# Key norm of the gated delta rule issued beside the value tiles' projections, value silus behind it

## Reference

```python
def gated_deltanet(q, k, v, z, a, b_logit, conv_w, a_log, dt_bias, norm_w):
    qkv = jax.nn.silu(causal_dwconv(jnp.concatenate([q, k, v], axis=-1), conv_w))
    q, k, v = jnp.split(qkv, 3, axis=-1)
    q = l2norm(to_chunks(q)) * D ** -0.5
    k = l2norm(to_chunks(k))
    v = to_chunks(v)
    ...
    sol = lax.linalg.triangular_solve(lower, rhs, left_side=True, lower=True, unit_diagonal=True)
    ...
    _, o = lax.scan(step, jnp.zeros((bsz, H, D, D), f32), xs)
```

## Time and profile before

| | us |
|---|---|
| timed runs | 3829.78, 3832.85, 3834.25 (median 3832.85) |
| the profiled execution's own time | 3828.58 |
| its span | 3826.8 |
| TensorE busy | 3475.4 (91% of the span) |
| VectorE / ScalarE / GpSimd busy | 47% / 34% / 11% |
| mean granted TensorE clock | 0.949 of full speed |
| mixer of the first layer, key norm's first sum to the last round's end | 1902.4 to 2093.5 |
| mixer of the second layer, the same | 2905.6 to 3093.5 |

### The profile page before, as it was taken

One profiled execution on the slowest core, in us unless ns is written; L12 is line 12 of the kernel. 1 busy time (PEld: TensorE's weight loads), 2 busy tenths in 40 slices (PEclk: granted clock), 3 DMA queues, 4 the chain that ended last, 5 costly groups with the idle time before them and its releaser, 6 DMA issues. The chain is left out here.

```text
span 3826.8 us, 46458 instructions
## 1 busy us (share of the span) xinstructions
PE 3475.4 (91%) x19317; PEld 2705.3 (71%) x19317; DVE 1780.1 (47%) x2762; ACT 1308.2 (34%) x2038; POOL 420.6 (11%) x351
## 2 busy tenths in 40 slices
PE   5989897999999789998897988999989988899998
PEld 4877765788777567886665756788766665577886
DVE  4775465443332534332544454444444444554534
ACT  2332353223232332322422353333333134533333
POOL 0001000120000101100023000221001310013100
PEclk7999998999999899999899999999989989999999
DMA  6651215333221032331301103232122020213231
GB/s 228 199 175 45 78 34 187 118 124 110 90 75 55 1 132 69 105 109 35 99 18 27 37 1 110 87 100 101 66 76 61 2 63 1 88 55 110 77 110 50
DMA packets 230575, 316.69 MB, mean 83 GB/s; under 512 B 13133, under 2 KB 167606, under 8 KB 229086
## 3 DMA queue, kind: packets, MB, share of 16 engines
q1 hardware_dynamic: 230366, 313.72, 24.9%
HBM read 311.04 MB, written 6.85 MB: 83 GB/s over the span
## 5 line engine op out<-in xcount | busy, mean ns | idle before, releaser
L493 PE MATMUL out<-h_lo,w_hi 128*128 128x512 f32 x2608 | 1043.1, 400 | 52.1 <-DVE w_lo L484 47.8
L494 PE MATMUL out<-h_hi,w_hi 128*128 128x512 f32 x2608 | 1022.2, 392 | 0.0
L495 PE MATMUL out<-h_hi,w_lo 128*128 128x512 f32 x2608 | 1021.6, 392 | 0.0
L484 DVE TENSOR_TENSOR w_lo<-ring,w_hi 128x1024 fp32r<-128x1024 f32 (+2 forms) x459 | 560.7, 1227 | 980.0 <-ACT w_hi L479 974.9
L479 ACT ACTIVATE w_hi<-ring 128x1024 fp32r<-128x1024 f32 (+2 forms) x459 | 469.2, 1027 | 1152.9 <-PE out L495 1061.1
L493 PEld LDWEIGHTS out<-h_lo,w_hi 128*128 128x128 f32 x2608 | 494.0, 189 | 178.1 <-issue 60.4
L494 PEld LDWEIGHTS out<-h_hi,w_hi 128*128 128x128 f32 x2608 | 493.8, 189 | 111.9 <-issue 11.0
L495 PEld LDWEIGHTS out<-h_hi,w_lo 128*128 128x128 f32 x2608 | 493.6, 189 | 103.9
L493 PE MATMUL item_banks<-h_lo,w_hi 128*128 128x512 f32 (+1 forms) x632 | 289.4, 458 | 14.3 <-DVE w_lo L484 5.1
L494 PE MATMUL item_banks<-h_hi,w_hi 128*128 128x512 f32 (+1 forms) x632 | 255.1, 404 | 0.0
L495 PE MATMUL item_banks<-h_hi,w_lo 128*128 128x512 f32 (+1 forms) x632 | 254.8, 403 | 0.0
(11 more groups left out here) (499 smaller groups left out, 4635.8 us busy)
## 6 DMA issues: line engine op xcount, KB each, us to landing
ring<-in_mlp_w SPq DMA_DIRECT2D x30, 2048.0 KB, 8.5
ring<-in_w_up SPq DMA_DIRECT2D x44, 1024.0 KB, 7.4
tiles<-in_mod_w SPq DMA_DIRECT2D x80, 512.0 KB, 4.6
ring<-in_e_w_in SPq DMA_DIRECT2D x48, 512.0 KB, 4.1
ring<-in_w_down SPq DMA_DIRECT2D x10, 2048.0 KB, 7.7
ring<-in_w_in SPq DMA_DIRECT2D x16, 1024.0 KB, 5.2
ring<-in_o_w_in SPq DMA_DIRECT2D x7, 2048.0 KB, 7.9
tiles<-in_mod_w SPq DMA_DIRECT2D x8, 1024.0 KB, 8.8
```

Of the source, the lines that this page charges most:

```text
L484: return nc.vector.tensor_tensor(lo.bitcast(F32R), x, hi, ALU.subtract)
L493: nc.tensor.matmul(out, wh, xl, start=start, stop=False, **kw)
L494: nc.tensor.matmul(out, wh, xh, start=False, stop=False, **kw)
L495: return nc.tensor.matmul(out, wl, xh, start=False, stop=stop, **kw)
```

## The change

Four numbers of the plan are changed. `DELTA` is 87.5 and no longer 94. The key norm begins 3.5 behind the last key item (67.9 and no longer 84.7) and is spread over 15.5 and no longer 9.0. The silus of the three value tiles are planned 3.0, 3.7 and 4.4 behind the last conv item, and no longer 3.0 behind each tile's own end. Since the item length changes from 5.6 to 9.4 at `DELTA`, the last item now ends at 167.6, and rotary follows at 168.6 (before 164.8). No arithmetic operation is added or taken away.

```diff
@@ Item.__init__
-        self.begin, self.length = 0.0, 0.0
+        self.begin, self.length, self.silu_at = 0.0, 0.0, None
@@ items_lane, ScalarE
-                steps += [(end, 2, m), (end + 3.0, 3, m)]
+                steps += [(end, 2, m), (end + 3.0 if item.silu_at is None else item.silu_at, 3, m)]
@@ second_mixer
-        BEGIN, DELTA, ROUND = 18.0, 94.0, 28.0
+        BEGIN, DELTA, ROUND = 18.0, 87.5, 28.0
...
+        keys_end, conv_end = (items[TC + n * GDN_T - 1].begin + items[TC + n * GDN_T - 1].length for n in (2, 3))
+        for t in range(GDN_T):
+            items[TC + 2 * GDN_T + t].silu_at = conv_end + 3.0 + 0.7 * t
...
-            conv_end = items[12].begin + items[12].length
-            normed = key_norm_lane(k, r, r.lane(conv_end + 3.5, 9.0),
+            normed = key_norm_lane(k, r, r.lane(keys_end + 3.5, 15.5),
```

## The result

| | us |
|---|---|
| kernel before, 20 runs beside the changed one | 3830.6 median (3828.3 to 3837.7) |
| changed kernel, 20 runs | 3838.61 median (3830.7 to 3848.8) |
| ratio, 95% interval | 1.0017 [1.0010, 1.0024], that is +6.5 us [3.8, 9.2] |
| profiled execution: own time, span | 3839.29, 3837.5 |
| TensorE busy, mean granted clock | 3485.9 (91%), 0.944 |

The change made the kernel slightly slower: +6.5 us where I had forecast -3.1 (+6.5 is the ratio times 3830.6; the two medians themselves differ by 8.0). The time lies inside the forecast range, its sign is the other one. I had written that a difference under 7.7 us can't be told from none; with 20 runs of each kernel this one can.

A forecast was written before the change was run, and what follows sets the result against it. TensorE, with its waits and the low clock behind them, was taken as the bound. Layer sums of -2.4 and -0.7 gave -3.1 us together, from 3831.4 to 3828.3; range 3817 to 3841.

The forecast's parts named there:

- R2: Second round of the delta rule: first L3373's wait falls from 2.87 to about 2.6, clock regained; -2.9 us per layer.
- R1: First round of the delta rule: TensorE's wait grows to about 3.1 us at low clock; +1.5 first layer, +3.2 second.
- Up to the delta rule: Key norm stretch before the first round: waits of 2.2 and 3.8 us; the round begins 6.4 us earlier per layer.
- Value silus: ScalarE's silus behind the last value tile: table loads hidden, taken as zero; upper bound 5.1 us over both layers.
- R3 and R4: Third and fourth delta rule rounds: triples added, rotary swaps moved, GpSimd products ahead of masks; +1.6 and +3.8 us per layer.
- A: Rival, 0.26: shift pays; fifth sum and first round keep the clock, fourth round's turns half hidden; -15.5 us, 3816.
- B: Rival, 0.18: fourth round's level one or two waits on GpSimd for a rotary product at low clock; +10.7 us, 3842.
- C: Rival: norm not hidden, L3333 waits for scales or silus; +4.2 us, 3832.5; chance 0.56 together with the forecast.

## Why the prediction was wrong

**The failing step is R2.** I wrote that the split moves the same way, but "L3373 comes at 12.3 and not 12.6, and the wait falls from 2.87 to about 2.6", and took -2.9 with a regained clock. L3373 came at 13.3 after a wait of 3.6 and at the low clock: +0.6. That is 7.0 of the 9.5 us between forecast and traces. Two terms of the forecast failed in it, as the stretches of R2 show. The wait: TensorE's idle time in R2 grew by 1.4 us (2.87 to 4.24) and did not fall by 0.3. The clock: its busy time fell by 0.8 (42.59 to 41.80, granted clock 0.92 to 0.96) and not by the 2.65 that I took for a clock fully regained.

For the wait I had moved the split with its old duration. In its new place it shares the time with GpSimd's masks, and L484 and L3506 took 0.5 and 0.4 more (1.75 and 1.74 for 1.23 and 1.35), which is 0.9 of the 1.0 us between 12.3 and 13.3. The 12.3 itself had no working in the prediction. That the split's place costs R1 and R2 their time is shown by moving it alone. That GpSimd's work is what lengthens it is read from rows and not tested by an edit, but the whole trace bears it out: all 380 splits of this size that meet no GpSimd instruction take 1.21 to 1.23 us, and every longer one runs beside one.

**R1** was right in mechanism and size (+1.8 and +3.6 for +1.5 and +3.2); its wait was 3.6 and not 3.1, since L3506 took 1.74 there too.

**Up to the delta rule.** Waits of 2.06 and 3.71 for 2.2 and 3.8, 33.7 and 33.8 for 33.8 us, no wait at L3333: right, and the -6.4 of the first layer too. In the second layer it was -4.9: there I let the clock cost half, as before, and it cost the whole (33.8 us in both layers). That guess cost 1.5.

**Value silus.** Hidden, as taken. The first exponential of R1 starts 1.24 us behind L3333 where it was 1.10, held by a table load:

```profile
1922.95 1.28 ACT L3450 ACT_TABLE_LOAD   x1
1924.25 0.49 ACT L3450 ACTIVATE delta_scratch<-delta_banks 128x384 f32<-128x384 f32 x1
```

(These are ScalarE's rows of the changed kernel, first layer.) The Trainium skill (ScalarE: Activation LUTs, What ACT_TABLE_LOAD costs) would have made this about 1 us late; no row here shows the drain that it adds to the load, and in the kernel with silus among the roots L551 starts 0.01 us behind its load's end. The measurement decides: 1.28 to 1.30 for a switch.

**R3 and R4.** +0.6 and +4.9 for +1.6 and +3.8. The sum was right (+5.4 forecast, +5.5 measured) by luck, since the two errors of one cancel. R3's +1.6 was the middle of a range of 0 to 3.2, not a forecast from rows. VectorE in R4 of the changed kernel, first layer:

```profile
2074.53 1.40 DVE L3598 TENSOR_TENSOR tiles<-tiles 128x512 f32<-128x512 f32 x1 [2.01 <-POOL tiles L3586]
2075.84 1.00 DVE L3524 TENSOR_TENSOR delta_scratch<-delta_scratch,delta_banks 128x384 f32<-128x384 f32 x2
...
2078.40 0.69 DVE L3598 TENSOR_TENSOR tiles<-tiles 128x512 f32<-128x512 f32 x1 [0.78 <-POOL tiles L3586]
2079.01 1.02 DVE L3524 TENSOR_TENSOR delta_scratch<-delta_scratch,delta_banks 128x384 f32<-128x384 f32 x2
```

L3524 stands behind L3598, which waits for GpSimd, as said. The second level's came at 2079.01 - 2059.49 = 19.5 and not 18.5; the first of these additions took 1.40 beside GpSimd's work where I took 0.6. (Of R4's four products on GpSimd in this trace, two stand among the masks from L3302 on, one ahead of L3300 and one behind L3314; the text on the change counts three among them.)

**Rivals.** A did not come: the fifth sum waited and lost the clock. B did not come in this kernel, but nearly with `DELTA` 0.8 earlier or 0.9 later. C did not come. No rival had R2 get longer. Nor did I see that the split could be worth more than the whole change, though its wait stood in the earlier trace rows.

## What to carry to other kernels

When a plan's offset moves, list what each shifted instruction now stands in front of, on the engine whose result the bound engine waits for next, and give it the duration that it has beside the work running there then. An operation that nobody needs soon (here a weight split for a later item) belongs behind the short chain that opens the next stage: moving it by two places in the changed kernel took 8 us out of each layer, where moving the whole norm alone had changed both layers together by 1.3. Where the bound engine has work on both sides of a border, as TensorE here, starting the later stage earlier gained nothing; look for its waits, and for the low clock behind them.

## What the runs showed of the hardware

- VectorE and GpSimd slow each other in some operations. In the changed kernel's trace the 380 L484 of 128 x 1024 that meet no GpSimd instruction took 1.21 to 1.23; beside L3310 they took 1.32 and 1.75 (2.01 with the split moved). L3506, always beside GpSimd, took 1.34 to 1.81 (0.95 in R2 with the split moved); L3598 0.69 to 1.40; five L3310 6.3 or 7.3. L3499, with one operand from `delta_banks`, kept its 0.61 beside them, and L560 its 0.68. The Trainium skill (SBUF — State Buffer, SBUF: two separate sides) says that only VectorE operations with two SBUF inputs (against a GpSimd operation that reads SBUF) or in a two-port mode exclude GpSimd's; these rows agree in which operations lengthen.
- The length of a wait does not alone decide about the clock. R1's first level waited 2.45 us in the kernel before (second layer) and with the norm alone, with the same order around it; R1 took 45.0 in one and 46.4 in the other, and R2 45.5 and 44.1. In the one the whole loss of clock fell into R2 (granted 1.00 and 0.92), in the other it was divided (0.96 and 0.96), and the two together were 90.5 in both.
